# VectorE splits one more weight chunk between freeing a tile's accumulators and turning its blocks

## The reference

```python
# first block
h = rms_norm(x, norm_in_g);  proj = h @ w_in      # q, k, v, z of two attentions, q and z of a third, gates
qa, ka, qb, kb = rope(qa), rope(ka), rope(qb), rope(kb)
ya = moba_attention(qa, ka, va) * silu(za)        # with 256 tokens: plain causal attention, 8 heads
yb = dilated_mixture(qb, kb, vb) * silu(zb)       # 3 groups of 4 heads
ym = memory_attention(qm, mk, mv) * silu(zm)      # mk, mv = rms_norm(mem) @ w_mem_kv
merged = g_a*(ya @ w_proj_a) + g_b*(yb @ w_proj_b) + g_m*(ym @ w_proj_m)
x = rms_norm(x + merged @ w_out, norm_final_g)
# second block
u = rmsnorm(x);  lru_x, lru_g, q, k, v, ret_g = split(u @ w_in_2)
y = concat(rg_lru(conv(lru_x)) * gelu(lru_g), retention(rope(q), rope(k), v, ret_g))
h = x + y @ w_out_2
h = h + (silu(rmsnorm(h) @ w_ffn_gate) * (rmsnorm(h) @ w_ffn_up)) @ w_ffn_down
out = rmsnorm(h, final_norm_w)
```

## Time and profile before

| what | us |
|---|---|
| median of 3 runs | 2202.65 |
| the profiled execution | 2204.24 |
| its span, first to last instruction | 2202.4 |
| TensorE (PE) matmul busy | 2185.7 (99%) |
| VectorE (DVE) busy | 1308.7 (59%) |
| ScalarE (ACT) busy | 1025.3 (47%) |
| GpSimd (POOL) busy | 144.2 (7%) |
| DMA engines, all queues, rate | 211 GB/s |

### The profile page before, as it was taken

One profiled execution on the slowest core, in us unless ns is written; L12 is line 12 of the kernel. 1 busy time (PEld: TensorE's weight loads), 2 busy tenths in 40 slices (PEclk: granted clock), 3 DMA queues, 4 the chain that ended last, 5 costly groups with the idle time before them and its releaser, 6 DMA issues.

```text
span 2202.4 us, 26200 instructions
## 1 busy us (share of the span) xinstructions
PE 2185.7 (99%) x9906; PEld 1811.4 (82%) x9906; DVE 1308.7 (59%) x1646; ACT 1025.3 (47%) x1235; POOL 144.2 (7%) x242
## 2 busy tenths in 40 slices
PE   9999999999999999999999999999999999999998
PEld 7888888887888888888888888888888888888886
DVE  5655656666455645546676878665555555554454
ACT  5544444443444444444554666454444444444443
POOL 0010101011000000000111100110001000100000
PEclk9999999999999999999999999999999999999999
DMA  8775656567754657667778756586777777776664
GB/s 293 219 230 177 203 164 214 182 225 220 219 163 148 211 177 229 201 204 282 228 259 249 229 182 200 192 247 210 211 211 225 220 211 211 227 236 193 194 194 146
DMA packets 228673, 464.65 MB, mean 211 GB/s; under 512 B 16344, under 2 KB 16608, under 8 KB 227680
## 3 DMA queue, kind: packets, MB, share of 16 engines
q1 hardware_dynamic: 212128, 408.73, 59.9%
q0 software_dynamic: 15712, 53.49, 8.0%
q10 hardware_dynamic: 736, 1.12, 0.1%
HBM read 437.59 MB, written 25.69 MB: 210 GB/s over the span
## 4 chain that ended last, share of the span: by engine, by line
PE 90%; DVE 4%; DMA 3%; ACT 1%; issue 1%; POOL 0%; POOLq 0%; ACTq 0%; DVEq 0%
PE ps L1485 29%; PE ps L1487 29%; PE ps L1486 29%; DVE w_lo L861 1%; DMA stage<-bounce 1%; PE ps L1345 1%; ACT w_hi L575 1%; PE ps L1376 1%; PE ps L1398 1%; DMA bounce<-tmp 1%; DVE tmp L1023 1%; DVE tmp L1014 0%; DVE stage L1009 0%; DVE stage L1018 0%; DMA raw<-in_w_out 0%
## 5 line engine op out<-in xcount | busy, mean ns | idle before, releaser
L861 DVE TENSOR_TENSOR w_lo<-raw,w_hi 128x1024 fp32r<-128x1024 f32 (+1 forms) x776 | 931.5, 1211 | 766.8 <-ACT w_hi L575 764.9
L575 ACT ACTIVATE w_hi<-raw 128x1024 fp32r<-128x1024 f32 (+1 forms) x776 | 810.3, 1050 | 917.2 <-PE ps L1487 824.5
L1485 PE MATMUL ps<-w_hi,xT_hi 128*128 128x512 f32 x1088 | 430.2, 395 | 1.6 <-DVE w_lo L861 1.6
L1487 PE MATMUL ps<-w_hi,xT_lo 128*128 128x512 f32 x1088 | 424.2, 390 | 0.0
L1486 PE MATMUL ps<-w_lo,xT_hi 128*128 128x512 f32 x1088 | 423.6, 389 | 0.0
L1485 PE MATMUL ps<-w_hi,u2T_hi 128*128 128x512 f32 x704 | 274.0, 389 | 0.0
L1487 PE MATMUL ps<-w_hi,u2T_lo 128*128 128x512 f32 x704 | 273.9, 389 | 0.0
L1486 PE MATMUL ps<-w_lo,u2T_hi 128*128 128x512 f32 x704 | 273.9, 389 | 0.0
L1485 PEld LDWEIGHTS ps<-w_hi,xT_hi 128*128 128x128 f32 x1088 | 204.4, 188 | 44.1 <-DVE w_lo L861 3.3
L1487 PEld LDWEIGHTS ps<-w_hi,xT_lo 128*128 128x128 f32 x1088 | 204.2, 188 | 43.5
L1486 PEld LDWEIGHTS ps<-w_lo,xT_hi 128*128 128x128 f32 x1088 | 204.5, 188 | 40.7
(11 more groups left out here) (262 smaller groups left out, 2259.3 us busy)
## 6 DMA issues: line engine op xcount, KB each, us to landing
raw<-in_w_in SPq DMA_DIRECT2D x368, 512.0 KB, 4.5
raw<-in_w_ffn_gate SPq DMA_DIRECT2D x88, 512.0 KB, 4.3
raw<-in_w_ffn_up SPq DMA_DIRECT2D x88, 512.0 KB, 4.5
raw<-in_w_ffn_down SPq DMA_DIRECT2D x88, 512.0 KB, 4.0
raw<-in_w_out SPq DMA_DIRECT2D x64, 512.0 KB, 5.1
bounce<-tmp POOLq DMA_DIRECT2D x41, 512.0 KB, 3.3
stage<-bounce POOLq DMA_DIRECT2D x164, 128.0 KB, 5.3
raw<-in_w_mem_kv SPq DMA_DIRECT2D x32, 512.0 KB, 5.7
```

The costliest lines, as they stand in the source:

```text
L575: nc.scalar.activation(w_hi[:, s, 0:per], raw[:, s, 0:per], ACT.Copy).then_inc(hi_ready, 1)
L861: nc.vector.tensor_tensor(w_lo[:, s, 0:per], raw[:, s, 0:per], w_hi[:, s, 0:per].bitcast(F32), ALU.subtract)\
L1485: nc.tensor.matmul(bank(2 * par + t), x_hi, w_hi[:, s, k], start=first, stop=False)
L1487: ins = nc.tensor.matmul(bank(2 * par + t), x_lo, w_hi[:, s, k], start=False, stop=last)
```

## The change

- `rotate` no longer adds `tmp` to `stage`, and rotary and `res`/`"u"` tiles no longer turn their blocks in `post`. A new function `turn_later` does both, one chunk later: in chunk 6 of a unit tile, else in chunk 4. In between, VectorE splits that chunk's weights.
- `late_in` gives 3 for all rotary tiles, so their turned blocks are copied out in chunk 3; the mark `"late"` goes away.
- `ret_decay(4)` moves from VectorE's chunk 4 to its chunk 3 of `tiles_out2`.
- At the end VectorE scales three of the four pieces and SyncE stores them; ScalarE scales and stores only the last one.

```diff
         def late_in(tile, late):
-            return 9 if len(chunks(tile)) > 9 else 3 if late and (late[0][1] or late[0][0][0] in ("res", "turn") or late[0][0][0] == "rope" and late[0][0][-1] == "late") else 1
+            return 9 if len(chunks(tile)) > 9 else 3 if late and (late[0][1] or late[0][0][0] in ("res", "turn", "rope")) else 1
...
             for t in range(NT):
-                for m in range(2):
-                    sp.wait_ge(rows_scaled, 2 * t + m + 1)
+                for m in range(NG - 1):
+                    sp.wait_ge(rows_scaled, (NG - 1) * t + m + 1)
...
-                for m in range(2, NG):
-                    c = slice(m * NW, (m + 1) * NW)
-                    if m == NG - 1:
-                        act.wait_ge(out_scaled, NG + t)
-                    nc.scalar.activation(h2[:, t, c], h2[:, t, c], ACT.Copy, scale=R["out"]["r"][:, t:t + 1]).then_inc(out_made[t], 1)
-                    act.wait_ge(out_made[t], m - 1)
-                    act.dma_start(out[t * P:(t + 1) * P, c], h2[:, t, c]).then_inc(stored, 16)
+                act.wait_ge(out_scaled, NG + t)
+                nc.scalar.activation(h2[:, t, cs], h2[:, t, cs], ACT.Copy, scale=R["out"]["r"][:, t:t + 1]).then_inc(out_made[t], 1)
+                act.wait_ge(out_made[t], 1)
+                act.dma_start(out[t * P:(t + 1) * P, cs], h2[:, t, cs]).then_inc(stored, 16)
...
                 last.then_inc(acc_free[par], 1)
-                dve.wait_ge(acc_free[par], w(f"a{par}", 1))
-                link(nc.vector.tensor_tensor(stage[:, :, :], stage[:, :, :], tmp[:, :, :], ALU.add))
...
+            def turn_later(prev):
+
+                kind, par = prev["post"], prev["par"]
+                if kind[0] == "rope":
+                    dve.wait_ge(acc_free[par], w(f"a{par}"))
+                    link(nc.vector.tensor_tensor(stage[:, :, :], stage[:, :, :], tmp[:, :, :], ALU.add))
+                    turn_blocks()
+                elif kind[0] == "res" and kind[3] == "u" and bounced(kind):
+                    dve.wait_ge(row_made, kind[2] + 1)
+                    turn_blocks()
...
-                if bounced(kind) and kind[0] != "res":
+                if bounced(kind) and kind[0] not in ("res", "rope"):
                     turn_blocks()
...
                         if what == "u":
                             last.then_inc(row_made, 1)
-                            dve.wait_ge(row_made, n + 1)
-                            turn_blocks()
...
                     if h == pos(tile, 5 if unit else 3):
                         post(prev, h + 1)
+                    if prev and h == (6 if unit else 4):
+                        turn_later(prev)
...
-                4: [lambda: ret_decay(4)], 5: [lambda: ret_norm(4)],
+                3: [lambda: ret_decay(4)], 5: [lambda: ret_norm(4)],
...
-                for m in range(2):
+                for m in range(NG - 1):
                     c = slice(m * NW, (m + 1) * NW)
                     nc.vector.tensor_scalar(h2[:, t, c], h2[:, t, c], R["out"]["r"][:, t:t + 1], None, ALU.mult).then_inc(rows_scaled, 1)
```

More of the change, by code:

```diff
@@ L364, in tiles_two @@
                 c = 2048 + half * NW
-                out_ += [dict(w=w_in2, col=c, x="u", post=("rope", qrT[half], 0, "late")),
-                         dict(w=w_in2, col=c + 1024, x="u", post=("rope", krT[half], 0, "late")),
+                out_ += [dict(w=w_in2, col=c, x="u", post=("rope", qrT[half], 0)),
+                         dict(w=w_in2, col=c + 1024, x="u", post=("rope", krT[half], 0)),
                          dict(w=w_in2, col=c + 2048, x="u", post=("take", vr[half][:, :, :])),
```

## The result

| kernel | runs | median us | lowest to highest |
|---|---|---|---|
| before | 22 | 2202.53 | 2199.7 to 2205.29 |
| changed | 22 | 2206.53 | 2204.3 to 2208.71 |

The ratio of the times is 1.0018, with a 95% interval of 1.0012 to 1.0024. So the change makes the kernel slower by 4.0 us, and by the interval between 2.6 and 5.3. The prediction named 0.2% as the bound of what can be told from no change. With 22 runs of each the loss is told from none, though the ratio is just under that bound.

What follows compares the result with a forecast made beforehand. TensorE, busy 99% of the span, was taken as the bound, so only its waits could be won. Wins of 4.15 us against costs of 3.5 gave -0.65 on the 2202.65 median: 2202.0 us, range 2198.4 to 2205.6.

Steps and rivals of the forecast that it cites:

- unit tiles: Later blocks delay the unit tiles: 1.1 us in va1, 0.95 in za1, 1.16 in qb2, 0.3 in kb0; 3.5 us lost.
- rotary tiles without a unit: At kb1 and kb2, TensorE's two waits for w_lo both go: 1.7 us won.
- ret_decay: Without the split ahead of it, probsT is ready ahead of TensorE, whose wait goes: 0.8 us won.
- residual tiles: Transpositions move behind the w_lo that TensorE waits for: all 0.95 us won.
- the end: The last store is issued 0.78 us earlier; 0.7 us taken as won, lower bound 0.3.
- a net of -0.65 us: Whole kernel: costs of 3.5 us less wins of 4.15 us make it 0.65 us faster.
- the split's 1.16: In every rotary tile z_made comes one split later, 1.16 us, delaying the bounce and ScalarE's copy.
- rival B: In unit tiles, the read-back meets more loads, up to 3.0 us longer per bounce: 2211 us; chance 0.08.
- the copy in the next tile's chunk 3 doesn't wait for it now, and keeps some microseconds: First two residual tiles: the bounce comes 1.2 us later, but the copy still has microseconds to spare.
- rival C: In the kb tiles, wins turn into new waits: 2203.9 us; chance 0.17.
- Rival A: In unit tiles, a faster read-back absorbs the turn's delay and only the wins stay: 2198.5 us; chance 0.2.

Runs made afterwards that it cites:

- experiments 3 and 4: 3: the kernel before with the new end alone, 2203.02 us; 4: the kernel before, unchanged, profiled once more, 2202.95 us.
- experiments 2 and 11: 2: the kernel before with the late turn in unit tiles alone, 2208.74 us; 11: the changed kernel profiled a second time, 2206.69 us.
- experiment 7: The kernel before with late turn and chunk-3 copy in rotary tiles without a unit alone: 2201.08 us, before 2203.38, ratio 0.9991.
- experiment 5: The changed kernel with ScalarE's copy of bounced rotary blocks in chunk 4 of unit tiles, behind its split: 2200.73 us, before 2203.38, ratio 0.9989.

## Why the prediction was wrong

For the unit tiles, the rotary tiles without a unit and `ret_decay` the mechanism was as the prediction told it. For the residual tiles and the end it was not: two wins were counted that something else takes away. No term came out in the kernel's favour, and a net of -0.65 us out of two sums of about four had no room for that. The runs give each term by several profiles: for every stretch I take the mean over the profiles with the old order and over those with the new one.

| term | predicted | measured in profiles | of |
|---|---|---|---|
| unit tiles | +3.5 | +4.5 (1.59 to 6.07) | 6 and 3 profiles, copy in chunk 3 |
| rotary tiles without a unit | -1.7 | -1.6 (1.64 to 0) | 6 and 7 |
| residual tiles | -0.95 | +0.5 (0.57 to 1.07) | 7 and 6 |
| `ret_decay(4)` | -0.8 | -0.8 (0.81 to 0) | all |
| the end | -0.7 | 0 (8.84 in each) | all |
| sum | -0.65 | +2.6 | |

Of the 3.25 us between the sums, 1.45 lie with the residual tiles, 1.0 with the unit tiles and 0.7 with the end. The 1.45 are the least certain: the mean of the new order rests on two profiles with over 2.3 us, and the changed kernel's own two have 0 and 0.56.

**The unit tiles** are the cost that was put too low: "The sum of the costs: 1.1 + 0.95 + 1.16 + 0.3 = 3.5 us". The turn at once has 1.21 to 2.08 us of stalls there in six profiles, the late turn 5.55, 5.84 and 6.83. By tile, as differences of the means over these profiles, the cost is 1.4 in `va1` (1.1 predicted), 1.5 in `za1` (0.95), 0.8 in `qb2` (1.16) and 1.0 in `kb0` (0.3); `ka1` and `qb1` together win 0.25.

- The delay of the blocks is more than the split's 1.16. Over the four bounces ScalarE waits 0.46 us on average in three profiles with the turn at once (before, experiments 3 and 4), and 2.09 us in the three with the late turn (after, experiments 2 and 11), 1.63 more. Where it did not wait before, a lead was used up too, so the delay itself is larger still. The landings say by what: from the first issue of the read-back to the landing of its last part it takes 6.75 us on average over the four bounces of the eight profiles with the turn at once, and 7.38 over those of the five with the late turn. So the transfer itself is longer, and 1.16 and 0.63 make a delay of 1.8. That is rival B in a weak form: 0.6 us, where B had 3.0 and decided from 1.7. The Trainium skill, in "DMA: Bandwidth & Descriptors", "Queues, rings and completion order", has the queues share a DMA engine in turns, and the prediction took from it that the cost would be over 1.16 per bounce. The traces agree in the sign; they don't show what the packets did.
- The leads were taken from one execution. In `za1` a lead of 0.2 was subtracted; the wait for the exponentials there is 1.3 to 2.04 us in the three profiles. In `kb0` 0.3 was left of the 1.16, and the wait for `y_tok` is 0.88 to 0.91.
- In `qb2` the error goes the other way. The prediction had 0.86 grow to about 2.0. It stayed at 0.9, and the 0.86 of the earlier trace rows was itself of one execution: 0.2 or nothing in experiments 3 and 4. Against the mean of the six the cost is 0.8.

**The residual tiles** are the largest part of the miss. "So all 0.95 is won" rested on one stall in one execution; the repeated profile of before has none there. And two steps failed. What is late next was missing: ScalarE's `w_hi` stands behind its squares in either order, and at equal lateness this leaves 0.36 of the 0.95 us. And "the copy in the next tile's chunk 3 doesn't wait for it now, and keeps some microseconds" did not hold: with the late turn ScalarE waits there in all six profiles, and the next post comes 1 us later on average. The stretch has 0 to 1.06 us of stalls in the seven profiles with the old order, and 0 to 2.35 in the six with the new one. A small loss or nothing, and no gain.

**The end.** The stores are issued as predicted. The timeline of the changed kernel, second half of the tokens:

```profile
2198.68 1.28 DVE L1338 TENSOR_SCALAR h<-h,small 128x512 f32<-128x512 f32 x3 [0.45 <-POOL small L563]
...
2199.19 1.31 SPq L486 DMA_DIRECT2D out_dram<-h  x3
...
2199.43 0.34 ACTq L840 DMA_DIRECT2D out_dram<-h  x1
```

Scaling starts 3.16 us after the last matmul's start in both kernels. The third piece is scaled by 2198.68 + 1.28 = 2199.96, and SyncE's three issues are over at 2199.19 + 1.31 = 2200.50, 1.8 us after the start of the scaling. Before, the last issue began at 2198.89 and was over at 2199.23, 2.5 us after it. That is the 0.7 us of the prediction, and yet the kernel ends no earlier. Two things take it away. The first is the DMA engines. In 40 slices of the last 13 us of the changed kernel (busy tenths, then GB/s), the second burst of stores is full from its first slices on:

```profile
DMA  0000000069999999610000002999999992000000
GB/s 0 0 0 0 0 0 0 0 233 391 403 416 403 365 397 328 252 38 0 0 0 0 0 0 88 391 403 410 378 397 366 410 321 76 13 0 0 0 0 0
```

The same window of the kernel before has 320 to 400 GB/s over eight slices. Of the 0.7 us, 0.2 arrive: counted from the last matmul's start, the last packet ends at 7.73 to 7.75 us in the six profiles with the new end, and at 7.93 to 7.95 in the seven with the old one. The second is GpSimd. Its program closes with an instruction `DRAIN`, which is entered as the last root starts and is 6450 ns long in both kernels (the rows of before, then of after; duration, then start):

```profile
L130 POOLq DRAIN  x1: 6450/6450/6450, 2195.7 to 2195.7; - x1
L130 SPq DRAIN  x1: 7/7/7, 2202.1 to 2202.1; - x1
...
L130 POOLq DRAIN  x1: 6450/6450/6450, 2197.7 to 2197.7; - x1
L130 SPq DRAIN  x1: 7/7/7, 2203.9 to 2203.9; - x1
```

In all 13 profiles it ends 8.61 us after the last matmul's start, and the span ends at 8.84. SyncE, which waits for the stores, is through at 8.56 to 8.59 with the old end and at 8.36 to 8.39 with the new one. So GpSimd ends last in either kernel, and the 0.2 us that do arrive win nothing. The prediction saw that the stores share the engines and put 0.3 as the lower bound; zero was the bound to take. How long GpSimd's `DRAIN` would be behind an earlier root was not tried.

**What held.** The two `w_lo` waits at `kb1` and `kb2` are gone, rival C's new ones did not come, and experiment 7 times this part alone at 0 to 4 us faster. `ret_decay` gives its 0.8: `probsT` is ready ahead of TensorE in every profile with the new place. Rival A, that the delay is absorbed, is out by ScalarE's waits.

**The profiled execution.** The prediction set its sum against 2204.24 and then moved it to the median. But an execution that is 1.6 us above the median has stalls that the median has not, and it was these (`qb2`, the third residual tile) from which one gain and one missing cost were read.

**What stays open.** The table's sum is 2.6 us, the measured loss 4.0 (2.6 to 5.3). The 1.4 us between are just within the interval, and the profiles of these kernels show no further stretch with a steady difference. Part of it can lie in the choice of executions: the two profiled ones of the changed kernel took 0.4 and 1.9 us less than the medians of their runs, so they may have fewer stalls than the usual one. The start of the weight matmuls lies anywhere from 12.4 to 15.8 us, in kernels that do the same until then; three profiles of late turns are too few to say more. Why the read-back is 0.6 us longer when it is later, by which queue or load, was not tried.

## What to carry to other kernels

A wait that stands in an engine's program ahead of work for others costs by what is queued behind it. If its data must come later, move the wait behind the next urgent work as well: experiment 5 turned a loss of 4 us into a gain of 0.4 to 4.4 us with one number. Before a stall of under 1 us goes into a sum, see it in a second execution: two of those that the prediction used were gone or a quarter of their size the next time. And before an earlier store is counted as a win at the end, look at what else must end there: here the stores together fill the DMA engines, and another engine's closing instruction ends later than they do.

## What the runs showed of the hardware

- Four stores of 256 KB at the end move at 320 to 410 GB/s. With the last issue 0.7 us earlier, their last packet ends 0.2 us earlier (7.73 to 7.75 against 7.93 to 7.95 us after the last matmul's start).
- The span ends 8.84 us after the last matmul's start in all 13 profiles, to within 0.01 us. GpSimd's closing `DRAIN`, 6.45 us long, ends at 8.61 in each, after the stores have landed.
- A read-back of 512 KB from DRAM in four DMAs, under the weight loads, takes 6.0 to 8.1 us from its first issue to its last landing for the four bounces that unit tiles copy out, 7.2 to 10.1 for the three `kb` bounces and 9.1 to 11.3 for those of the residual tiles, while from 300 to 600 us the single DMAs' medians from issue to landing are 5.0 us (changed) and 4.9 (before). For the chain the first of these is the number to use.
- Executions of one program with no difference in the code move single stalls by 0.7 to 0.8 us: `qb2`'s `y_tok` wait is 0.86 and 0.2 in two profiles of the kernel before, a residual tile's is 0.79 and nothing, and `za1`'s wait for the exponentials in the changed kernel is 2.04 and 1.3.
